# First projection in two passes over ten and six feature blocks, with a quarter of the late w_ada rows on GpSimd

## The reference, cut to what matters

```
c_act = silu(c)                                   # 2048 numbers
mod = c_act @ w_ada + b_ada                       # w_ada is 2048 x 12288
sh1, sc1, gt1, sh2, sc2, gt2 = split(mod, 6)
h = rms_norm(x, g_mix) * (1 + sc1) + sh1          # 256 x 2048
z = h @ w_in                                      # w_in is 2048 x 11344
q_sb, k_sb, v_sb, q_ds, ... = split_columns(z)    # the first 3072 columns are q_sb, k_sb, v_sb
```

## Time and profile before

| what | us |
| --- | --- |
| median of 3 runs (lowest, highest) | 2701.59 (2701.42, 2702.1) |
| the profiled execution's own time | 2701.95 |
| its span | 2700.2 |
| PE busy | 2633.8 (98%) |
| PE weight loads | 2167.6 (80%) |
| DVE busy | 1790.5 (66%) |
| ACT busy | 1293.4 (48%) |
| POOL busy | 222.1 (8%) |

### The profile page before, as it was taken

One profiled execution on the slowest core, in us unless ns is written; L12 is line 12 of the kernel. 1 busy time (PEld: TensorE's weight loads), 2 busy tenths in 40 slices (PEclk: granted clock), 3 DMA queues, 4 the chain that ended last, 5 costly groups with the idle time before them and its releaser, 6 DMA issues.

```text
span 2700.2 us, 34387 instructions
## 1 busy us (share of the span) xinstructions
PE 2633.8 (98%) x12073; PEld 2167.6 (80%) x12073; DVE 1790.5 (66%) x2052; ACT 1293.4 (48%) x1563; POOL 222.1 (8%) x162
## 2 busy tenths in 40 slices
PE   1999999999999999999999999999999999999999
PEld 0788887888888888888888887877888888888887
DVE  7977776878778666666666855677555555555555
ACT  1445554455455444444444554555554444444443
POOL 0000000100000000000000310131001111111110
PEclk9999999999999999999999999999999999999999
DMA  9978777677886666666666556643666666666663
GB/s 396 384 253 299 256 268 237 220 249 260 309 280 226 204 202 203 203 204 204 204 202 188 188 168 184 184 141 125 197 185 193 188 192 188 190 190 190 190 191 136
DMA packets 280497, 585.49 MB, mean 217 GB/s; under 512 B 21760, under 2 KB 24220, under 8 KB 279508
## 3 DMA queue, kind: packets, MB, share of 16 engines
q1 hardware_dynamic: 280052, 583.54, 67.0%
q10 hardware_dynamic: 352, 0.71, 0.1%
HBM read 582.01 MB, written 2.11 MB: 216 GB/s over the span
## 4 chain that ended last, share of the span: by engine, by line
PE 94%; DVE 3%; DMA 2%; issue 1%; ACT 0%; SPq 0%; DVEq 0%; ACTq 0%
PE lin L464 29%; PE lin L466 29%; PE lin L465 29%; DMA sb_ada<-in_w_ada_dram 2%; DVE sb_acc L1681 1%; PE aux L768 1%; PE aux L498 1%; DVE sb_wlo L1586 1%; PE aux L779 0%; PE aux L952 0%; PE aux L464 0%; PE aux L466 0%; PE aux L465 0%; PE aux L521 0%; DVE sb_gm L2329 0%
## 5 line engine op out<-in xcount | busy, mean ns | idle before, releaser
L1586 DVE TENSOR_TENSOR sb_wlo<-sb_raw,sb_whi 128x1024 fp32r<-128x1024 f32 x896 | 1102.6, 1234 | 803.2 <-ACT sb_whi L1008 800.0
L1008 ACT ACTIVATE sb_whi<-sb_raw 128x1024 fp32r<-128x1024 f32 x896 | 948.1, 1060 | 1237.2 <-PE lin L466 1144.5
L464 PE MATMUL lin<-sb_whi,sb_act_hi 128*128 128x512 f32 x2720 | 1078.7, 397 | 2.0 <-DVE sb_wlo L1586 1.5
L466 PE MATMUL lin<-sb_whi,sb_act_lo 128*128 128x512 f32 x2720 | 1060.3, 390 | 0.0
L465 PE MATMUL lin<-sb_wlo,sb_act_hi 128*128 128x512 f32 x2720 | 1059.0, 389 | 0.0
L464 PEld LDWEIGHTS lin<-sb_whi,sb_act_hi 128*128 128x128 f32 x2720 | 510.9, 188 | 111.4 <-issue 9.4
L466 PEld LDWEIGHTS lin<-sb_whi,sb_act_lo 128*128 128x128 f32 x2720 | 510.5, 188 | 108.0
L465 PEld LDWEIGHTS lin<-sb_wlo,sb_act_hi 128*128 128x128 f32 x2720 | 511.2, 188 | 104.1 <-issue 2.6
L464 PE MATMUL lin<-sb_whi,sb_hid_hi 128*128 128x512 f32 x704 | 275.4, 391 | 0.0
L466 PE MATMUL lin<-sb_whi,sb_hid_lo 128*128 128x512 f32 x704 | 274.2, 389 | 0.0
L465 PE MATMUL lin<-sb_wlo,sb_hid_hi 128*128 128x512 f32 x704 | 273.9, 389 | 0.0
(11 more groups left out here) (353 smaller groups left out, 1663.3 us busy)
## 6 DMA issues: line engine op xcount, KB each, us to landing
sb_raw<-in_w_in_dram SPq DMA_DIRECT2D x176, 512.0 KB, 6.2
sb_raw<-in_ffn_w_gu_dram SPq DMA_DIRECT2D x176, 512.0 KB, 3.7
sb_ada_in<-in_w_ada_dram SPq DMA_DIRECT2D x128, 512.0 KB, 4.2
sb_raw<-in_gla_w_in_dram SPq DMA_DIRECT2D x96, 512.0 KB, 3.8
sb_raw<-in_w_gate_dram SPq DMA_DIRECT2D x88, 512.0 KB, 3.8
sb_raw<-in_w_up_dram SPq DMA_DIRECT2D x88, 512.0 KB, 4.4
...
```

Source lines behind the costliest of these rows:

```text
L464: pe.matmul(o, h, whi[:, w], start=first and q == 0, stop=False)
L466: m = pe.matmul(o, l, whi[:, w], start=False, stop=last and q == 1)
L1008: act.activation(whi[:, idx % RING * HALF:(idx % RING + 1) * HALF], raw[:, idx // 2 % RING, idx % 2 * HALF:(idx % 2 + 1) * HALF], ACT.Copy ...
L1586: dve.tensor_tensor(wlo[:, c], raw[:, idx // 2 % RING, idx % 2 * HALF:(idx % 2 + 1) * HALF], whi[:, c].bitcast(fp32), ALU.subtract).then_i ...
```

## The change

`EARLY` is now a number of feature blocks, 10 instead of 3 chunks of 4. Blocks 0 to 3 and 4 to 9 are summed early, blocks 10 to 15 late, in pieces of 128 x 1536 numbers (768 KB) with four slots of their own. SP issues the first four late pieces behind half 7, when all early sums are done, and each of the others once the piece four before it has been added. Rows 3, 7, 11 and 15 of the late pieces are multiplied and added by POOL, into an accumulator `acc2` of its own; DVE has the other twelve, after splits 5 to 23 (`LATE_AT`). PE sums `acc1` and `acc2` in one pass of two matmuls a column.

Phase A runs in two passes. The first has 30 halves: groups 3, 4, 5, 0, 1, 2, each over the five early pairs. Groups 3, 4, 5 are copied to `sbz`; 0, 1, 2 stay in PSUM. The second has 18 halves: groups 1, 0, 2, 3, 4, 5, each over the three late pairs. Groups 1, 0, 2 are copied out as before; for 3, 4, 5 DVE adds the banks to what is in `sbz` (`a_sum`). The late column sum stands after half 25, the late high and low parts behind split 28, the index projection after half 32. The other w_ada chunks start at slab 15 and come five in four slabs until slab 67. In the stick-breaking attention DVE's waits on `sb_own` become waits on `dve_link`.

```diff
-EARLY = 3
+EARLY = 10
+LATE = KT - EARLY
-    ("A", 1, 48, 6), ...
+    ("A", 1, 48, 9), ...
-EARLY_ROWS = KT - 1 + EARLY
+CHUNKS = ((0, 4), (4, EARLY), (EARLY, KT))
+EARLY_ROWS = KT + 1
+A_GROUPS = (3, 4, 5, 0, 1, 2)
+A_AGAIN = (1, 0, 2, 3, 4, 5)
+A_PAIRS = EARLY // 2
+A_ENDS = [6 * A_PAIRS + (KT // 2 - A_PAIRS) * (n + 1) for n in range(6)]
+A_HALVES = [(g, p) for g in A_GROUPS for p in range(A_PAIRS)] + [(g, p) for g in A_AGAIN for p in range(A_PAIRS, KT // 2)]
+SHARED = 4
+by_vector = lambda kt: kt - kt // SHARED
+LATE_AT = {}
+for _k in range(KT):
+    LATE_AT.setdefault(A_PAIRS + 4 * _k // 3, []).append(_k)
-    _at = 12 + _n * 11 // 19 if _n < 19 else 4 + _n if _n < 64 else ...
+    _at = 15 + _n if _n < 9 else 24 + (_n - 9) * 4 // 5 if _n < 64 else ...
...
@@ SP
         def late_piece(kt):
+            before = kt - SLOTS
+            if before >= 0 and before % SHARED == SHARED - 1:
+                sp.wait_ge(sem("pool_sum"), before // SHARED + 1)
+            else:
+                sp.wait_ge(sem("ada0_sum"), EARLY_ROWS if before < 0 else EARLY_ROWS + by_vector(before) + 1)
...
+        for i in range(48):
+            first_half(i)
+            if i == 2 * RING - 1:
+                for kt in range(SLOTS):
+                    late_piece(kt)
+            for kt in LATE_AT.get(i - 2 * RING, ()):
+                if kt + SLOTS < KT:
+                    late_piece(kt + SLOTS)
+            if i == 28:
+                sp.dma_start(ixw_raw[:]...
+            if i % 2:
+                for n in CHUNKS_AT.get(i // 2, ()):
+                    ada_chunk(n)
@@ PE
+        def first_columns(n):
+            k0, k1 = CHUNKS[n]
+            acc, c0, w = (acc1, 0, KT - EARLY) if n == 2 else (acc0, k0 * P, k1 - k0)
+            for j in range(2 * w):
+                c = c0 + j % w * P
+                o = aux[n % 2][:, j * WIDE // 2:(j + 1) * WIDE // 2]
+                m = pe.matmul(o, acc[:, j // w, c:c + P], ones[:, 0:WIDE // 2], start=True, stop=n < 2)
+                if n == 2:
+                    m = pe.matmul(o, acc2[:, j // w, c:c + P], ones[:, 0:WIDE // 2], start=False, stop=True)
...
+        drained_before = {A_PAIRS * 3: 3, A_PAIRS * 4: 4, A_PAIRS * 5: 5, A_ENDS[2]: 6, A_ENDS[3]: 7, A_ENDS[4]: 9}
+        for i, (g, p) in enumerate(A_HALVES):
+            again, held = i >= 6 * A_PAIRS, g in A_AGAIN[0:3]
+            if i in drained_before:
+                pe.wait_ge(free0, drained_before[i])
+                pe.wait_ge(free1, drained_before[i])
+            if g in (A_GROUPS[0], A_AGAIN[0]):
+                pe.wait_ge(sem("tt_lo"), p + 1)
+            half(0, "A", 48, i, g, 2 * p, ...)
+            if i == 5 * A_PAIRS:
+                pe.wait_ge(sem("ada0_sum"), EARLY_ROWS + by_vector(KT))
+                pe.wait_ge(sem("pool_sum"), KT // SHARED)
+                first_columns(2)
+            if i == A_ENDS[0] - 1:
+                project_ix()
...
@@ ACT
+        act.wait_ge(sem("gs_made"), 2)
+        for g in range(2, A_PAIRS):
+            first_pair(g)
...
@@ DVE
+        for g in range(2, A_PAIRS):
+            if g < RING:
+                split(0, "A", 48, g)
+            first_low(g, xT[:, 2 * g:2 * g + 2, :])
...
+        def a_sum(n):
+            g, banks = A_AGAIN[n], lin[(0, 0, 0, 1, 0, 1)[n]]
+            drained(0, "A", A_ENDS[n])
+            for tb, free in ((0, free0), (1, free1)):
+                dve.wait_ge(free, 2 + 3 + n)
+                z = sbz[:, tb, g * NB:(g + 1) * NB]
+                dve.tensor_tensor(z, banks[tb][:], z, ALU.add).then_inc(free, 1)
+        def late_low():
+            first_modulation(2)
+            dve.wait_ge(sem("gs_made"), 3)
+            for g in range(A_PAIRS, KT // 2):
+                first_affine(g)
+                first_low(g, xaff[:, g % 2, :, :])
+            dve.wait_ge(sem("tt_lo"), KT // 2)
...
+        for idx, kts in LATE_AT.items():
+            for kt in (kt for kt in kts if kt % SHARED < SHARED - 1):
+                hk.setdefault(idx, []).append(lambda kt=kt: late_add(kt))
+        hk.setdefault(28, []).append(late_low)
+        hk.setdefault(31, []).append(split_ix)
...
@@ POOL
+        pool.wait_ge(sem("tt_free"), KT // 2)
+        for n in range(KT // SHARED):
+            kt = SHARED * n + SHARED - 1
+            pool.wait_ge(sem(f"ada0_in{kt % SLOTS}"), 16 * (KT // SLOTS) + 16 * (kt // SLOTS) + 16)
+            acc, new = acc2[:].rearrange("p b n -> p (b n)"), ada1[:, kt % SLOTS, :]
+            if n == 0:
+                m = pool.tensor_scalar(acc, new, cact[:, kt:kt + 1], None, ALU.mult)
+            else:
+                pool.wait_ge(sem("pool_sum"), n)
+                link(pool.tensor_scalar(new, new, cact[:, kt:kt + 1], None, ALU.mult))
+                m = pool.tensor_tensor(acc, acc, new, ALU.add)
+            m.then_inc(sem("pool_sum"), 1)
```

More of the change, by code:

```diff
@@ L93, in build_program @@
     X = at("x", [P, TB, D], XB)
[L95 to L97 removed]
+    ada0 = at("ada0", [P, SLOTS, 2 * EARLY * P], ARENA)
+    ada1 = at("ada1", [P, SLOTS, 2 * LATE * P], ARENA + 24 * KB)
+    acc0 = at("acc0", [P, 2, EARLY * P], ADA)
+    acc1 = at("acc1", [P, 2, LATE * P], ADA + 10 * KB)
+    acc2 = at("acc2", [P, 2, LATE * P], XB + 8 * KB)
     xaff = at("xaff", [P, 2, 2, S], XB)
@@ L1741, in _ @@
                 norm_rows(X)
-        for kc in range(EARLY):
-            last_add(kc)
+        for n in range(2):
+            last_add(n)
         first_modulation(0)
```

172 lines of the change are left out of this document (59 added, 113 removed).

## The result

The changed kernel takes 2718.19 us, median of four runs (2716.08 to 2720.32), against 2701.51 for the kernel before beside it: 1.0061 of its time, 95% interval 1.005 to 1.0073. The profiled execution took 2716.08 us, the quickest of the four, with a span of 2714.3, 14.1 more than before. The forecast was 2701.9 and its range ended at 2709.5.

A forecast was written before the change was run, and what follows sets the result against it. PE was taken as full, so the time is its matmul stream plus the stretch before it. Terms -8.7 + 2.0 + 7.0 = +0.3 us on the profiled 2701.95 gave 2702.2, by median 2701.9; range 2694.0 to 2709.5.

The forecast's parts named there:

- Part 1: Early w_ada rows: ten blocks instead of twelve start PE's matmul stream at 71.0 instead of 79.68, -8.7 us.
- Part 2: Late column sum inside PE's stream: one sum of 48 instructions, 5.6 us, replaces two of 3.6 together, +2.0 us.
- Part 3: Phase A's two passes, drains and DVE's sums of groups 3, 4, 5: no wait for PE, nothing.
- Part 5: Late rows on DVE and POOL: POOL's 18.8 us count as DVE's time, PE waits in two or three holes, +7.0 us.
- Holes of 2 to 4 us I cost at nothing: PE's clock after holes behind POOL operations: no loss taken; a 10 us stretch at half speed would add 5.
- Part 4: Later w_ada chunks, 1.25 a slab until slab 67: DVE has room beside a slab's splits, nothing.
- The clock term: PE's clock lowered by idle holes: taken at nothing, though a 10 us stretch at half speed would add 5.
- dear multiply: Rival: POOL's multiply takes 3.9 us like an add, holes 15.5, 2710.4 us; sign a multiply of 3.2 or more; chance 0.13.
- the memset: Price of POOL's multiply by a column: taken as 2.0 us, nearer to a memset (1.4 from below) than an add (3.9).
- DVE not held: Rival: POOL's operations slip into DVE's own gaps, so PE has no hole, 2694.7 us; chance 0.26.
- the filler: Matmul between the second early column sum and PE's stream: its 1.08 us counted whole, from 69.9 to 71.0.

The follow-up runs named there:

- e2: The changed kernel with all sixteen late rows on DVE, none on POOL, one accumulator and 24 matmuls in the late column sum: 2702.30 us, ratio 1.0003.
- e4: The kernel before with only the new w_ada chunk table (five chunks in four slabs from slab 24 to 67): 2711.14 us, ratio 1.0036.
- e13: As e2, with one w_ada chunk moved, the second of slab 64 to slab 65: 2695.68 us, ratio 0.9978.
- e6: The changed kernel without POOL's multiplies and adds of rows 3, 7, 11, 15; the sum keeps 48 matmuls and reads acc1 twice: 2706.17 us, ratio 1.0017.
- e7: As e6, with the 48 matmuls of the late column sum in three parts behind halves 23, 24 and 25: 2704.24 us, ratio 1.0012.
- e8: The changed kernel with the four multiplies of POOL's rows on ACT, POOL only adding: 2706.52 us, ratio 1.0018.
- e5: As e2, but 64 w_ada chunks over slabs 15 to 67, two at 16, 18, 20, 22, 25, 29, 33, 37, 41, 45, 49, one elsewhere: 2701.35 us.

## Why the prediction was wrong

Its steps, against the profile of after (us):

| step | forecast | measured |
| --- | --- | --- |
| Part 1, the start | -8.7 | -10.0 |
| Part 2, column sums | +2.0 | +1.9 |
| Part 3, two passes and drains | 0 | 0 in e2 (B at -10.9) |
| Part 5, PE's waits behind POOL | +7.0 | +5.8 |
| Part 5, "Holes of 2 to 4 us I cost at nothing" | 0 | +6.8 |
| Part 4, "The w_ada chunks ... Nothing" | 0 | +9.4 |
| sum | +0.3 | +13.9 |

The time was 2718.19 by median for 2701.9. The profiled execution has 13.9 of the 16.7 us between the medians; the table prices these.

*Part 4 failed, and most.* I reckoned only DVE's time (a chunk and two splits, 3.5 of 5.44 us) and left out SP's queue, on which the chunk is issued ahead of the raw halves. A second chunk in one slab waits for DVE's add of the one two before it, and everything behind it waits too. e4 prices the table alone at 9.7 us, and e13 shows that one of its chunks is worth 6.6. In Part 5 I had named who stands behind SP's wait; here, for the same kind of wait, I did not.

*The clock term failed.* I named a price (a 10 us stretch at half speed adds 5) and took nothing, since the expected holes were short. There was one hole of 4.7, followed by 3.4 us at the lower level, and then 10.2 us more from the middle of the column sum on. That second one I had not thought of at all: a stream of PE that never stops, but of narrow matmuls. e6 and e7 part it from the hole: about 3.1 us of the 6.8 belong to the run of 48 alone, and the remainder goes with POOL's multiplies (e8 against after): about 1.7 right behind the hole, and about 2.0 in a longer stretch at the sum.

*Part 5's mechanism was right and its size near.* POOL and DVE exclude each other, and PE waited 5.8 us for forecast 7.0. The single terms were off in both directions: the multiplies held DVE for 2.2 to 3.0 where I took 2.0, the adds for 3.3 where I took 3.6, 20.1 in all for 18.8. PE's wait came out smaller than my sum makes of that, since the last multiply and add fell (139 to 146) where PE had split halves in hand. That the column sum began at 148.68 for my 149 is in part luck: the start was 1.3 us early and the waits 1.2 short, and the clock, which I had at nothing, took 1.7 before the sum. The waits stood ahead of the column sum and on splits, as forecast, in one hole of 4.7 and a short one of 1.1 for "two or three". The rival "dear multiply" came half true: a POOL multiply's record is 4.6 us where it is least disturbed (118.38), over the 3.2 that I named as its sign and at least as long as an add's, so the memset was the wrong neighbour for its price. But it holds DVE for 3.0 at most, and the holes were 5.8, not 15.5; that its time, 2710.4, lies nearer to the result has other causes. "DVE not held" fell with the earlier trace rows confirmed; its 2694.7 also lacks the 0.4 us that the forecast takes off. The rule of the Trainium skill that I named there (SBUF — State Buffer, "Who interferes with whom") agrees with after's rows: 4.77 instead of 1.80.

*Part 1 was right with 1.3 us in hand*: 0.7 because the last early row was taken up at 62.47 and not at 63.2, and 0.5 because the filler starts at 69.15 and the first half's matmul at 69.69, where I had counted the filler's whole 1.08. The second sum took its 2.6 as forecast. The same start came at -8.8 to -10.0 in the other profiles, so the difference is about as large as their spread.

What the edit gives in itself was there: e13 has ten early blocks, two passes, all rows on DVE, and a chunk table with its worst place mended, and is 5.9 us faster than the kernel before (0.9978 of its time, interval 0.9968 to 0.9987). The rows on GpSimd were not needed, since e2's DVE has no hole with all sixteen.

Open: which doubles in B cost how much. Doubles at 25, 29, ... cost 8 us (seven), at 28, 32, ... 5 (six), at 24, 28, ... 2.5 and 3.6 (eight, e2 and e13), and the waits that PE shows explain only part (5.5 of 8 in e5). One table of eight doubles costs 2.3 to 4.7 us in B over the eight profiles that have it, so the number of doubles doesn't order these losses, and what their place does is hard to tell from that spread. That ScalarE, waiting for a raw slab, holds up the attention's steps behind it is argued from its waits and not shown. Also open is why the runs of the variants spread more than those of the kernel before.
